# Seven pairs per layer in seven block products, f cut in later pairs, and sums of weights made at other stages

## What is computed

```python
def conv_ffn(h, w_up, conv_w, conv_b, w_down):
    Tp = h.shape[1]
    u = h @ w_up                     # 1024 -> 5632
    up = jnp.pad(u, ((0, 0), (CONV_W - 1, 0), (0, 0)))
    c = conv_b + sum(up[:, j:j + Tp] * conv_w[j] for j in range(CONV_W))   # CONV_W = 3
    gate, val = jnp.split(c, 2, axis=-1)
    return (jax.nn.silu(gate) * val) @ w_down      # 2816 -> 1024
```

## Time and profile before

| | |
|---|---|
| median of 3 runs | 2134.62 us (2134.41 to 2135.7) |
| the profiled execution | 2133.73 us |
| its span, first to last instruction | 2132.4 us |
| mean granted TensorE clock | 0.998 |
| busy, share of the span | TensorE 98%, its weight loads 87%, VectorE 71%, ScalarE 48%, GpSimd 8% |
| first and last RWKV output (os 0, os 7) | 269.5 and 598.0 us |
| up products of layer 0 and of layer 1 | 1077 to 1329 us, 1759 to 2007 us |
| GpSimd's sums of weights | 270.5 to 390 us and 1074 to 1198 us |
| GpSimd's memsets of TZ behind them | 832.2 us and 1471.3 us |

### The profile page before, as it was taken

One profiled execution on the slowest core, in us unless ns is written; L12 is line 12 of the kernel. 1 busy time (PEld: TensorE's weight loads), 2 busy tenths in 40 slices (PEclk: granted clock), 3 DMA queues, 4 the chain that ended last, 5 costly groups with the idle time before them and its releaser, 6 DMA issues.

```text
span 2132.4 us, 45270 instructions
## 1 busy us (share of the span) xinstructions
PE 2098.8 (98%) x19690; PEld 1849.1 (87%) x19690; DVE 1506.8 (71%) x2534; ACT 1033.8 (48%) x1787; POOL 174.5 (8%) x171
## 2 busy tenths in 40 slices
PE   7999999999999999999999999999999999999999
PEld 2877777788777888898899999999988899999987
DVE  5889887888698766985589886324666668897622
ACT  4225555656442635355565554224666656554311
POOL 0000011000000002364321000000000030000000
PEclk9999999999999999999999999999999999999999
DMA  7631055321223353100177632223111033443231
GB/s 299 130 118 51 3 142 153 83 75 47 102 88 99 117 186 116 60 23 23 52 202 207 179 119 85 92 92 130 61 44 32 21 95 95 129 139 100 83 108 67
DMA packets 68566, 215.72 MB, mean 101 GB/s; under 512 B 8240, under 2 KB 11312, under 8 KB 68048
## 3 DMA queue, kind: packets, MB, share of 16 engines
q1 hardware_dynamic: 62128, 189.24, 27.7%
q0 software_dynamic: 6240, 23.60, 5.0%
HBM read 206.18 MB, written 30.21 MB: 111 GB/s over the span
## 4 chain that ended last, share of the span: by engine, by line
PE 80%; DVE 14%; ACT 3%; issue 2%; DMA 1%; SPq 0%; DVEq 0%; ACTq 0%
PE PS L638 60%; DVE wlo L2120 3%; PE PS L823 3%; DVE ca L2222 2%; PE PS L812 2%; PE PS L1370 2%; PE PS L1185 2%; PE PS L1338 1%; PE PS L1237 1%; PE PS L832 1%; ACT whi L1418 1%; DVE sq L2765 1%; PE PS L1158 1%; DVE sq L2760 1%; DVE Ssc L2639 1%
## 5 line engine op out<-in xcount | busy, mean ns | idle before, releaser
L1418 ACT ACTIVATE whi<-raw 128x1024 fp32r<-128x1024 f32 (+3 forms) x338 | 322.9, 956 | 205.9 <-PE PS L638 200.0
L2120 DVE TENSOR_TENSOR wlo<-raw,whi 128x1024 fp32r<-128x1024 f32 (+2 forms) x280 | 330.2, 1186 | 94.6 <-ACT whi L1418 94.3
L638 PE MATMUL PS<-nhi,whi 128*128 128x264 f32 (+1 forms) x1744 | 366.0, 291 | 0.3 <-DVE nlo L2488 0.3
L638 PE MATMUL PS<-nhi,wlo 128*128 128x264 f32 (+1 forms) x1744 | 353.2, 284 | 0.4 <-DVE wlo L2120 0.4
L638 PE MATMUL PS<-nlo,whi 128*128 128x264 f32 (+1 forms) x1744 | 353.4, 284 | 0.0
L638 PEld LDWEIGHTS PS<-nhi,whi 128*128 128x128 f32 x1744 | 271.3, 190 | 7.8 <-issue 1.1
L638 PEld LDWEIGHTS PS<-nhi,wlo 128*128 128x128 f32 x1744 | 270.8, 189 | 0.7 <-DVE wlo L2120 0.6
L638 PEld LDWEIGHTS PS<-nlo,whi 128*128 128x128 f32 x1744 | 271.2, 189 | 0.0
L638 PE MATMUL PS<-hhi,whi 128*128 128x512 f32 x648 | 265.7, 410 | 1.0 <-DVE hlo L2175 0.4
L638 PE MATMUL PS<-hhi,wlo 128*128 128x512 f32 x648 | 255.4, 394 | 0.5 <-DVE wlo L2120 0.4
L638 PE MATMUL PS<-hlo,whi 128*128 128x512 f32 x648 | 254.0, 392 | 0.0
(11 more groups left out here) (410 smaller groups left out, 3925.6 us busy)
## 6 DMA issues: line engine op xcount, KB each, us to landing
raw<-in_wall SPq DMA_DIRECT2D x256, 512.0 KB, 3.7
p_rows<-in_wall POOLq DMA_DIRECT2D x10, 1280.0 KB, 6.9
raw<-p_rows SPq DMA_DIRECT2D x20, 512.0 KB, 4.3
early<-in_wall SPq DMA_DIRECT2D x16, 512.0 KB, 14.9
raw<-in_wall SPq DMA_DIRECT2D x16, 384.0 KB, 3.1
p_rows<-in_wall POOLq DMA_DIRECT2D x20, 256.0 KB, 5.8
p_rows<-p_rows POOLq DMA_DIRECT2D x20, 256.0 KB, 4.4
raw<-in_wall SPq DMA_DIRECT2D x20, 256.0 KB, 2.6
```

The source lines that it names most:

```text
L638: q = e.matmul(out, cuts[a][:, k * P:(k + 1) * P], (hi_, lo_)[b][:, kr, lo:lo + w], start=start and k == 0 and a == b == 0, stop=stop and ...
L1418: return e.activation(out, src, func, **kw)
L2120: e.tensor_tensor(wlo[slot[i]][:, w], room_of(i)[:, w], whi[slot[i]][:, w].bitcast(F32), ALU.subtract).then_inc(*up("lo_dve", i))
```

## The change

- `SEVENTHS` has pairs 5, 7, 9, 11, 13, 15 and 17 in each layer.
- `gated` writes f whole into `f_whole`, which is the memory of flo, now 23 tiles, tile j in place (j + 3) mod 23 (`slot_of`); `f_lower` subtracts in place. V2 is free once the product is made. The helpers of the block products have other places in fhi and flo, and the waits before tiles 6 and 14 are now one before tiles 9 and up.
- `split_by` says up to which tile f is cut at each half pair: tiles 0 to 4 as they come, none in pairs 5 to 17, then two tiles in each half of pairs 18 to 21, and the last three behind them. VectorE follows half a pair behind ScalarE.
- The cuts of weights that stand ahead of a block pair move forward: ScalarE's before the second first tap, VectorE's right behind the second eviction (before: between the two taps).
- The down product begins with its blocks 0 and 1 in turn: unit for f tiles 0 to 7 of both, then 8 to 15, then 16 to 21.
- The small step for lambda moves from pairs 14 to 18 of layer 0 to pairs 1 to 3.
- GpSimd makes the sums of three quads behind the last RWKV output (os 7), and of the other eleven where `sums_of(1)` stood.
- The code for two block pairs in a row (`again`) isn't reached, as no two of the pairs are neighbours.

```diff
-SEVENTHS = ((5, 7, 9, 11, 13), (5, 7, 9, 11, 13))
+SEVENTHS = ((5, 7, 9, 11, 13, 15, 17), (5, 7, 9, 11, 13, 15, 17))
...
-        for j in range(8):
+        for js in ((0, 1), (2,), (3,), (4,), (5,), (6,), (7,)):
             for k0, nk in ((0, 8), (8, 8), (16, 6)):
-                units.append((f"down{layer}", j * P, k0, nk))
+                for j in js:
+                    units.append((f"down{layer}", j * P, k0, nk))
...
+        f_whole = grid(sb("f_whole", common + 22 * T * 4, 23 * T), 23)
...
+        def slot_of(j):
+            return (j + 3) % 23
...
+        def split_by(layer, j, n):
+            after = j - 1 - SEVENTHS[layer][-1]
+            if after < 0:
+                return min(j, SEVENTHS[layer][0])
+            return min(j, SEVENTHS[layer][0] + (2 * after + n + 1) * (22 - SEVENTHS[layer][0]) // (2 * (21 - SEVENTHS[layer][-1])))
...
-                    if layer == 0 and j == 16:
+                    if layer == 0 and j == 2:
                         on.wait_ge(*at("lam_pr"))
...
                     if j:
-                        on.wait_ge(*(at(f"f{layer}", j - 1) if n else at("f_gated", layer, j - 1)))
+                        on.wait_ge(*at("f_gated", layer, j - 1))
...
-                def f_upper(j):
-                    on.wait_ge(*at("f_gated", layer, j))
-                    if j == 6:
-                        on.wait_ge(*at("T_lo", layer, 3))
-                    if j == 14:
-                        on.wait_ge(*at("unit", last_sum))
-                    act(fhi[layer][:, j, c:], V2[1][:, c:], ACT.Copy).then_inc(*up("f_hi", layer, j))
+                def f_upper(upto):
+                    while split[0] < upto:
+                        j = split[0]
+                        split[0] += 1
+                        on.wait_ge(*at("f_gated", layer, j))
+                        if j >= 9:
+                            on.wait_ge(*at("unit", last_sum))
+                        act(fhi[layer][:, j, c:], f_whole[:, slot_of(j), c:], ACT.Copy).then_inc(*up("f_hi", layer, j))
...
                     ahead(count.take() + 3)
-                    f_upper(j - 1)
                     ahead(count.take() + 3)
...
                     normed()
-                    if j:
-                        f_upper(j - 1)
                     tap0(j, 0)
                     operands(j, 0)
+                    f_upper(split_by(layer, j, 0))
                     normed()
                     gate(j)
-                    tap0(j, 1)
                     if j + 1 in SEVENTHS[layer]:
                         ahead(count.next + 3)
+                    tap0(j, 1)
+                    f_upper(split_by(layer, j, 1))
...
-                    if n and j + 1 in SEVENTHS[layer] and j not in SEVENTHS[layer]:
+                    if j + 1 in SEVENTHS[layer] and j in SEVENTHS[layer] and n == 0:
                         ahead(count.next + 3)
...
-                    f_lower(j - 1)
                     i = count.take()
...
                         evac(U0[layer][n][:, 2 + c0:2 + T], b, i, "U", layer, j, n, n=(T, LATE)[layer])
-                        if j and n == 0:
-                            f_lower(j - 1)
+                        if j + 1 in SEVENTHS[layer] and n:
+                            ahead(count.next + 3)
+                        f_lower(split_by(layer, j if n else j - 1, 1 - n))
...
-            on.wait_ge(*at("os", 0))
-            sums_of(0)
+            on.wait_ge(*at("os", 7))
+            sums(0, 3)
...
-            sums_of(1)
+            sums(3, len(quads))
```

More of the change, by code:

```diff
@@ L637, in product @@
                         for n, (out, lo, w) in enumerate(outs):
-                            q = e.matmul(out, cuts[a][:, k * P:(k + 1) * P], (hi_, lo_)[b][:, kr, lo:lo + w],
+                            q = e.matmul(out, cuts[a][:, k * P:(k + 1) * P], (hi_, lo_)[b][:, kr if b == 0 or what[:4] != "down" else slot_of(kr), lo:lo + w],
                                          start=start and k == 0 and a == b == 0, stop=stop and k == nk - 1 and a == 1)
@@ L1208, in residual @@
             def residual(what, name, hi_, lo_, rhs, n, n_units=1, first=0):
-                for j in range(8):
+                if n_units == 3:
+                    b = {}
+                    for c in range(3):
+                        for j in range(2):
+                            if c == 0:
+                                b[j] = pair_of_banks((name, j))
+                            full(what, hi_, lo_, halves(n, b[j], T - n), (lambda k: on.wait_ge(*at(rhs, k))) if j == 0 else None,
+                                 start=(c == 0), stop=(c == 2), k0=8 * c)
+                for j in range(2 if n_units == 3 else 0, 8):
                     b = pair_of_banks((name, j))
@@ L1219, in sevenths @@
                 w, c0 = ((T, LATE)[layer]) // 2, T - (T, LATE)[layer]
-                pair = 2 * ((turn2[0] + 1) % 2)
-                bank_of = {1: 4, 2: 5, 6: 6, 5: pair + 1, 7: 7, 4: pair, 3: 4}
+                pair, other = 2 * ((turn2[0] + 1) % 2), 2 * (turn2[0] % 2)
+                again = j - 1 in SEVENTHS[layer]
+                bank_of = {1: other, 7: other + 1, 3: 7} if again else {1: 4, 7: 7, 3: 4}
+                bank_of.update({2: 5, 6: 6, 5: pair + 1, 4: pair})
+                banks["sum", layer, j] = bank_of
                 def whole(r, t):
@@ L1877, in residual @@
                 for j in range(8):
-                    for _ in range(n_units):
+                    for _ in range({0: 5, 1: 1}.get(j, 3) if n_units == 3 else 1):
                         passed()
@@ L1933, in sevenths @@
                         on.wait_ge(*at("M126", layer, max(x for x in SEVENTHS[layer] if x < j)))
-                    act(M1[:, 0:w], PS[:, 4, 0:w], ACT.Copy).then_inc(*up("M1", layer, j))
+                    act(M1[:, 0:w], PS[:, banks["sum", layer, j][1], 0:w], ACT.Copy).then_inc(*up("M1", layer, j))
                     ahead(count.take() + 3)
-                    f_upper(j - 1)
                     ahead(count.take() + 3)
@@ L2737, in residual @@
                     b = a_pair()
-                    for _ in range(n_units - 1):
+                    for _ in range({0: 4, 1: 0}.get(j, 2) if n_units == 3 else 0):
                         passed()
@@ L2802, in sevenths @@
                     ahead(i + 3)
-                    pair = 2 * ((turn2[0] + 1) % 2)
+                    bank_of = banks["sum", layer, j]
+                    pair = bank_of[4]
                     gate_2 = uv_[0][:, w:2 * w]
@@ L3047, in gpsimd, with sums @@
             e.memset(u[:, :, 0:30], 0.0).then_inc(*up("u_zero"))
-            def sums_of(layer):
-                for q, (of, j) in enumerate(quads):
-                    if of != layer:
-                        continue
+            def sums(first_quad, upto):
+                for q in range(first_quad, upto):
                     first = wall[tail + q * QUAD:tail + (q + 1) * QUAD]
```

56 lines of the change are left out of this document (34 added, 22 removed).

## The result

The changed kernel took 2124.07 us (median of 4 runs, 2121.36 to 2126.59), the kernel before 2134.51 us beside it (4 runs). The ratio is 0.9948, with a 95% interval of 0.9936 to 0.9961: 8 to 14 us faster, against a forecast of 11.5 us. The profiled execution took 2124.4 us, its span is 2123.1 us (before: 2132.4).

A forecast was written before the change was run, and what follows sets the result against it. TensorE, busy 98% of the span, was taken as the bound, with VectorE binding too among the seven-block pairs. Terms 5.9 + 1.9 + 3.7 = 11.5 us off 2133.7 give 2122.2, as a median 2123.1 us; range 2120.5 to 2128.7.

The forecast's parts named there:

- The pairs: Up products: two more pairs in seven blocks per layer, 1.48 us less TensorE time for each, -5.9 us in all.
- The stalls in pairs 11 and 13: Up products: TensorE's waits for late lower weights go, 0.94 us in layer 0 and the same in layer 1, -1.9 us.
- VectorE's need: Up products: VectorE's time for two pairs, said to fall from 22.43 to 20.7 us.
- the reserve: Up products: VectorE needs 20.7 us for two pairs against TensorE's 21.88, so it no longer falls behind.
- The tail: Pairs 18 to 21: VectorE with the late cuts of f needs 10.2 to 11.4 us a pair, under 11.68; cost 0.
- my second rival: VectorE sets the pace in the tail, or pairs 11 to 17 still stall: 2125 to 2129 us, chance 0.14.
- The order of the down units and the lambda step: Down product's first units in turn, and lambda's small step moved from pair 16 to pair 2: 0 each.
- The stall in the RWKV stage: At 350 us TensorE's program arrives late behind a bulk copy; moving the copies removes stall and lower clock, -3.7 us.
- the bounds that I gave: For the stall at 350 us: 0 if it has another cause, to -4.2 us with the 29 matmuls between.

The follow-up runs named there:

- Experiment 7: The changed kernel with only pairs 5, 7, 9, 11 and 13 in seven blocks per layer: 2129.1 us, ratio 0.9963 to the kernel before.
- Experiment 8: The changed kernel with the cuts of weights ahead of a block pair back in their old places: 2122.69 us, ratio 0.9940 to the kernel before.
- experiment 11: The changed kernel with an eighth block pair (19) in each layer: 2121.43 us, ratio 0.9934 to the kernel before.
- experiment 10: The changed kernel with the down product's units in the old order: 2122.2 us, ratio 0.9932 to the kernel before.
- experiment 1: The kernel before with the five sums behind the first RWKV output moved behind the last: 2130.0 against 2136.65 us, ratio 0.9973.
- experiments 3: The kernel before with each of the five bulk copies behind the first RWKV output made three times: 2141.87 against 2136.65 us, ratio 1.0027.
- experiment 4: The kernel before with each of the five bulk copies from 1074 us on made three times: 2136.11 against 2135.95 us, ratio 1.0000.

## Why the prediction was right, and where it was off

The forecast was 2123.1 us and the measurement 2124.07. The terms of the change held in their mechanism, but that the sum came so close is in part luck. The stages of the two profiles add up as 5.9 (pairs) + 2.0 (stalls) + 5.2 (the sums of weights, up to the fourth RWKV output) = 13.1 us of gain. Against it stand 0.5 us of the down product, which no term held, and 3.3 us in parts whose length varies (the first 270 us, outputs 4 to 8 and the stretch to the up products), which leaves the 9.3 us between the spans. The timed runs say 8 to 14.

*The pairs* (-5.9 us). Experiment 7 gives 3.01 + 2.93 = 5.9 us. A matmul taken from a TensorE that doesn't wait is worth its distance to the next, and nothing fell off on the way.

*The stalls in pairs 11 and 13* (-1.9 us, layer 1 taken as layer 0). 1.11 + 0.90 = 2.0 us by experiment 7, which has the lambda step and the late cuts in it too. (Only the rows at 1231.04 and 1910.96 us name "DVE wlo"; the one at 1208.61 us has no bracket, and its stall is read from the starts.) VectorE's need was put too low: 20.7 us for two pairs, while it is about 21.85 - 0.53 = 21.3 us (the row at 1209.70 us). I had not counted that inside the block pair it waits for whi, 0.45 us at 1207.94 us. The sign of the reserve was right, its size half. Experiment 8 says the same from the other side: without the moved cuts the reserve is nil.

*The tail* (0). Right: 9.98 us for a pair against 11.68, below the 10.2 that I had worked out. But experiment 11 shows where the reserve ends, and my second rival had named the right place (weights, not evictions) only in passing.

*The order of the down units and the lambda step* (0 each). Right by experiment 10 and by the stages: the time from the down product of layer 0 to the up products of layer 1 is the same to 0.03 us.

*The stall in the RWKV stage* (-3.7 us). The mechanism held, and the term was too small, because it priced one of two losses. The stall at 350 us with what followed it cost 53.31 - 49.15 = 4.2 us, which is the far end of the bounds that I gave. The other 1.1 us fell between the first two outputs, near 309 us, with no stall in the chain that stands out (the largest is 0.64 us), and I had no term for it. Together 5.2 us, and 5.6 in the second profile of the same five sums; the timed runs of experiment 1 say 5.8 (3.8 to 7.7). The two ends of the stage, 598.0 and 594.9 us, differ by only 3.1, as its later part happened to be 1.9 us shorter in the profile of before. That TensorE's program is what comes late is shown by its packets: the one that is due beside the bulk copy at 345 us began as the copy ended. And the same copies stall TensorE at 21 matmuls per us and not at 8 (experiments 3 and 4), with "issue" as the releaser each time. The Trainium skill (Runtime: NRT & Kernel Launch, Instruction fetch mechanics) has the cost of a block's boundary "mostly hidden"; by experiments 3 and 4 that holds among the up products and not in the RWKV stage beside copies between DRAM tensors.

*What no term held.* The down product of layer 1 is 0.54 us longer, in every kernel that keeps f whole (122.30 to 122.32 us; 123.73 in experiment 11, with its late weights) and in none that doesn't (121.76 to 121.77). It is spread over all 528 matmuls, one per 0.2321 us in place of 0.2311, with no wait of TensorE in either. In layer 0 (264 columns) the same product is 0.1 us longer. It isn't the order (experiment 10); that the place of flo in memory has to do with it was not tried, and the cause stays open. And 1.2 us went between the RWKV stage and the up products. That stretch took 478.6 to 479.3 us in the six profiles without sums at its start and 478.6 to 479.9 us in the eight with them, 0.3 us more on average, so most of the 1.2 us is its spread; what three sums at 595 us cost there wasn't isolated.

## What to carry to other kernels

A second engine that is a few per cent slower than the bound engine over a stretch is paid only where its cushion ends: compare the two periods over the stretch, before adding more of what loads both. Work that can wait (here the cuts of f) belongs in a stretch where that engine has room, but not right behind the stretch in which it falls behind. A background transfer is free or not by what the busy engine does beside it: place it where few instructions per microsecond are taken. Price it by timed runs, or by the same stretch in several profiles, from a mark ahead of it to a mark behind it: one stall in one chain showed 2.5 of 5.2 us.

## What the runs showed of the hardware that I had not expected

TensorE's program comes by DMA, in packets of 16 KB for 254 instructions, and a copy between DRAM tensors can hold one up: the packet due near 346 us began at 350.3 us, behind a copy of 1280 KB, and TensorE stood still for 2.54 us. Such stalls of 0.8 to 2.5 us, with "issue" as the only reason, came in stretches with 21 small matmuls per us; some of up to 1.05 us came there without any copy. Ten more copies of 1280 KB cost 5 us there and nothing (ratio 1.0000, 0.9991 to 1.0009) where TensorE takes 8 matmuls per us.

The stall of 2.54 us was followed by the lower clock (0.50 at 353 us), which made it cost more than its length. One of 2.28 us in experiment 4 was not (1.00 from 368 to 372 us). And a 512-column matmul took 0.2321 us in place of 0.2311 in one layout of an operand and not in the other; the cause is open.
